# Hybrid encoder step on one core: the attention mask as one fp32r matmul, and the output projection's second column half token tile by token tile

## What is computed

```
x = x + 1/2 * SwiGLU_1(RMSNorm(x))
P = RMSNorm(x) @ w_in
A = gated delta rule, 4 heads of 128 (blocks of 128 tokens, then the streams)
B = softmax(q1 k1) v - lambda * softmax(q2 k2) v, 4 heads, two maps of dim 64 each
    prompt: a query of 64-token chunk c sees the keys of chunks 0..c
x = x + concat(A, B) @ w_out          (1024 x 1024)
x = x + 1/2 * SwiGLU_2(RMSNorm(x))
```

## Time and profile before

| | |
|---|---|
| median of three runs | 1503.07 us |
| the profiled execution | 1500.5 us, of which the span is 1498.7 us |
| mean granted clock of TensorE | 0.975 of full speed |
| busy: PE, VectorE, ScalarE, GpSimd | 1404.1, 914.1, 668.4, 360.7 us (94, 61, 45, 24%) |
| attention and delta rule, scores of the prompt | 774.6 to 875 us of the span |
| output projection | 993.4 to 1052.1 us |
| first product of the second FFN | 1061.57 us |

### The profile page before, as it was taken

How to read it: one execution, slowest core, us unless ns; L and a number is a source line. 1 busy time by engine, 2 the same in 40 slices (tenths; PEclk the granted TensorE clock), 3 DMA queues, 4 the chain that set the end, 5 groups by cost and what they waited for, 6 DMA issues and landing times.

```text
span 1498.7 us, 24413 instructions
## 1 busy us (share of the span) xinstructions
PE 1404.1 (94%) x8709; PEld 1259.7 (84%) x8709; DVE 914.1 (61%) x1485; ACT 668.4 (45%) x1253; POOL 360.7 (24%) x240
## 2 busy tenths in 40 slices
PE   5999999999997999999988988779899999999999
PEld 5999999988886997787877665467799999998887
DVE  4976677644446676647636665643787777654444
ACT  6555555533334544434243332442655555543333
POOL 0645555300000000312022221000265555530000
PEclk9999999999998999999998999899999999999999
DMA  6223332270102422101030025580112222235000
GB/s 191 63 88 91 89 92 86 84 267 0 28 0 60 126 79 64 57 30 56 33 124 1 1 76 187 185 297 1 57 57 85 84 84 84 84 108 228 6 30 35
DMA packets 139254, 127.27 MB, mean 85 GB/s; under 512 B 3781, under 2 KB 107845, under 8 KB 139196
## 3 DMA queue, kind: packets, MB, share of 16 engines
q1 hardware_dynamic: 136684, 117.15, 24.4%
q0 software_dynamic: 2512, 9.34, 1.8%
HBM read 115.83 MB, written 10.39 MB: 84 GB/s over the span
## 4 chain that ended last, share of the span: by engine, by line
PE 83%; DVE 11%; ACT 3%; issue 2%; DMA 1%; POOL 0%; SPq 0%; DVEq 0%; ACTq 0%
PE psum_all L898 22%; PE psum_all L899 21%; PE psum_all L900 21%; PE psum_all L908 6%; PE psum_all L1756 2%; DVE hw_lo L329 1%; PE psum_all L1769 1%; PE psum_all L2003 1%; PE psum_all L2006 1%; PE psum_all L1872 1%; PE psum_all L1761 1%; DMA x_tok<-x_prompt 1%; DVE x_norm L423 0%; PE psum_all L472 0%; DMA K_c<-cache_k 0%
## 5 line engine op out<-in xcount | busy, mean ns | idle before, releaser
L898 PE MATMUL psum_all<-hw_hi,gu_op 128*128 128x320 f32 x1200 | 375.6, 313 | 12.3 <-DVE gu_op L554 4.7
L899 PE MATMUL psum_all<-hw_lo,gu_op 128*128 128x320 f32 x1200 | 372.7, 311 | 0.0
L900 PE MATMUL psum_all<-hw_hi,gu_op 128*128 128x320 f32 x1200 | 372.3, 310 | 0.0
L898 PEld LDWEIGHTS psum_all<-hw_hi,gu_op 128*128 128x128 f32 x1200 | 228.3, 190 | 13.3 <-issue 8.9
L899 PEld LDWEIGHTS psum_all<-hw_lo,gu_op 128*128 128x128 f32 x1200 | 228.3, 190 | 0.0
L900 PEld LDWEIGHTS psum_all<-hw_hi,gu_op 128*128 128x128 f32 x1200 | 228.1, 190 | 0.0
L554 DVE TENSOR_TENSOR gu_op<-w_sum,gu_op 128x512 fp32r<-128x512 f32 x160 | 161.0, 1007 | 55.7 <-ACT gu_op L550 50.9
L779 POOL TENSOR_TENSOR w_sum<-raw_gu 128x512 f32<-128x512 f32 x80 | 137.8, 1722 | 214.0 <-DVE gu_op L554 210.8
L898 PE MATMUL psum_all<-wd_hi,a_hi 128*128 128x512 f32 x440 | 171.4, 390 | 1.7 <-DVE x_tok L916 1.7
L900 PE MATMUL psum_all<-wd_hi,a_lo 128*128 128x512 f32 x440 | 171.2, 389 | 0.0
L899 PE MATMUL psum_all<-wd_lo,a_hi 128*128 128x512 f32 x440 | 171.2, 389 | 0.0
(11 more groups left out here) (349 smaller groups left out, 2500.1 us busy)
## 6 DMA issues: line engine op xcount, KB each, us to landing
raw_gu<-ffn_w_gu SPq DMA_DIRECT2D x80, 512.0 KB, 4.6
wd<-ffn_w_down SPq DMA_DIRECT2D x2, 4096.0 KB, 20.9
raw_b<-w_in SPq DMA_DIRECT2D x8, 1024.0 KB, 5.3
K_c<-cache_k SPq DMA_DIRECT2D x8, 1024.0 KB, 8.1
V_c<-cache_v SPq DMA_DIRECT2D x8, 1024.0 KB, 5.5
wd<-ffn_w_down SPq DMA_DIRECT2D x2, 3584.0 KB, 11.9
raw_cv<-w_in SPq DMA_DIRECT2D x13, 512.0 KB, 4.0
wd<-ffn_w_down SPq DMA_DIRECT2D x6, 1024.0 KB, 5.0
```

The costliest lines, as they stand in the source:

```text
L898: nc.tensor.matmul(out, lhs_hi, rhs_hi, start=start, stop=False, skip_group_check=True)
L899: nc.tensor.matmul(out, lhs_hi, rhs_lo, start=False, stop=False, skip_group_check=True)
L900: return nc.tensor.matmul(out, lhs_lo, rhs_hi, start=False, stop=stop, skip_group_check=True)
```

## The change

The mask's operands become two fp32r tiles made once by ScalarE, and the mask is one fp32r matmul over the same 64 rows as the scores (the 64 rows add up to -6.4e31). The concatenated heads get tiles of their own, laid out by token tile (`mixed_hi`, `mixed_lo`, over the same memory as `hT_hi`, `hT_lo`). The first column half of the projection stays as it was. All weights of the second half are kept split (seven blocks in `keep_o`, the eighth in `o_hi[0]`), made in an order that interleaves them with the first half's (SPLITS); the second half then runs token tile by token tile, eight blocks of weights each, with the norm transposes of a tile behind the product of the next. The norm's steps on ScalarE and VectorE go in turn, tile by tile.

```diff
-            square(0)
-            square(1)
-            root(0)
-            square(2)
-            root(1)
-            root(2)
-            columns(0, 4)
+            if in_turn:
+                square(0)
+                root(0)
+                square(1)
+                root(1)
+                columns(0, 2)
+                square(2)
+                root(2)
+                columns(2, 4)
...
+            if in_turn:
+                dve.wait_ge(gain_ready, 16)
+                for t in range(3):
+                    residual(t)
+                    inverse(t)
+                    scale(t)
...
             token_lo(dve, f, 0)
             token_lo(dve, f, 1)
+            if in_turn:
+                residual(3)
             token_lo(dve, f, 2)
             token_lo(dve, f, 3)
...
+        late = Region(nc, gain_at + 4096, small.at)
+        late_neg = late.put("late_neg", [P, P], F32R)
+        late_one = late.put("late_one", [P, DK], F32R)
...
+            nc.scalar.activation(late_neg[:], const("early_neg"), ACT.Copy)\
+                .then_inc(N["qkT_copied"], 1)
+            nc.scalar.activation(late_one[:], const("ones")[:, 0:DK], ACT.Copy)\
+                .then_inc(N["qkT_copied"], 1)
...
-                    last = nc.tensor.matmul(psum[m][:, n - 64:n], const("early_neg")[0:1, :],
-                                            const("lvl64")[0:1, 64:P], start=False, stop=True,
+                    last = nc.tensor.matmul(psum[m][:, n - 64:n], late_neg[rows, :],
+                                            late_one[rows, :], start=False, stop=True,
...
+        SPLITS = [(0, 0), (0, 1), (0, 2), (1, 0), (0, 3), (1, 1), (0, 4), (1, 2), (0, 5), (1, 3),
+                  (0, 6), (1, 4), (0, 7), (1, 5), (1, 6), (1, 7)]
...
+            for half, k in SPLITS:
+                if half == 0:
+                    if k == 2:
+                        finish(diff_out_act(act, 1))
+                    for m in BEHIND.get(k - 2, ()):
+                        out_act(act, m)
+                    if k >= 2:
+                        act.wait_ge(N["wo_step"], k - 1)
+                elif k == 0:
+                    act.wait_ge(*on.tr(2 * TT))
+                elif k >= 5:
+                    act.wait_ge(N["wo_lo"], NTH_SPLIT[0, k if k == KT - 1 else 4])
+                    if k == KT - 1:
+                        act.wait_ge(N["wo_step"], KT - 1)
                 act.wait_ge(s_wo[half], 16)
-                nc.scalar.activation(o_hi[:, n % 2], raw_o[half][:, k, :], ACT.Copy)\
+                nc.scalar.activation(out_weights(half, k)[0], raw_o[half][:, k, :], ACT.Copy)\
                     .then_inc(N["wo_hi"], 1)
...
+            dve.wait_ge(N["x_back"], 32)
+            for t in range(TT):
+                wout_residual(dve, 0, t)
...
+        def late_bank(t):
+
+            return (7, 0, 1, 0, 1)[t]
...
+            for t in range(TT):
+                if t:
+                    pe.wait_ge(N["wo_res"], (0, 1, 2, TT + 2, TT + 3)[t])
+                for k in range(KT):
+                    if t == 0:
+                        pe.wait_ge(N["wo_lo"], NTH_SPLIT[1, k])
+                    last = three(psum[late_bank(t)], mixed_hi[:, t, k], mixed_lo[:, t, k],
+                                 *out_weights(1, k), k == 0, k == KT - 1)
+                last.then_inc(N["wo_out"], 1)
+                if 1 <= t <= 3:
+                    norm_pe(pe, f2.n, (t - 1,), f2.hx)
...
             wout_pe(pe)
-            norm_pe(pe, f2.n, range(3), f2.hx)
             ffn_pe(pe, f2)
```

More of the change, by code:

```diff
@@ L343, in columns @@
                         .then_inc(f.hx.sem, 1)
-            square(0)
-            square(1)
-            root(0)
-            square(2)
-            root(1)
-            root(2)
-            columns(0, 4)
+            if in_turn:
[7 more added lines that the diff above has]
+                columns(2, 4)
+            else:
+                square(0)
+                square(1)
+                root(0)
+                square(2)
+                root(1)
+                root(2)
+                columns(0, 4)
             token_hi(act, f, 0)
@@ L365, in ffn_norm_act, with ffn_norm_dve @@
             token_hi(act, f, 5)
-        def ffn_norm_dve(dve, f, gain_ready, residual=lambda t: None, ahead=lambda dve: None):
+        def ffn_norm_dve(dve, f, gain_ready, residual=lambda t: None, ahead=lambda dve: None,
+                         in_turn=False):
             s = f.n
@@ L370, in ffn_norm_dve @@
             scale = lambda t: norm_scale(dve, s, t)
[L371 to L381, removed]
+            if in_turn:
[4 more added lines that the diff above has]
+                    scale(t)
+            else:
+                residual(0)
+                residual(1)
+                inverse(0)
+                residual(2)
+                inverse(1)
+                dve.wait_ge(gain_ready, 16)
+                scale(0)
+                inverse(2)
+                scale(1)
+                scale(2)
+                residual(3)
             token_lo(dve, f, 0)
             token_lo(dve, f, 1)
+            if in_turn:
+                residual(3)
             token_lo(dve, f, 2)
@@ L2354, in out_hT @@
             half, t = n // TT, n % TT
-            part = which[:, 4 * half:4 * half + 4, t * P:(t + 1) * P]
+            part = which[:, t, 4 * half:4 * half + 4, :]
             return part if n < 2 * TT - 1 else part.rearrange("p h (b c) -> p h b c", c=32)
@@ L2376, in out_act, with out_weights @@
             act.wait_ge(*on.tr(n + 1))
-            nc.scalar.activation(out_hT(hT_hi, n), out_psum(n), ACT.Copy).then_inc(on.hi.sem, 1)
+            nc.scalar.activation(out_hT(mixed_hi, n), out_psum(n), ACT.Copy).then_inc(on.hi.sem, 1)
         def out_dve(dve, n):
             dve.wait_ge(*on.hi(n + 1))
-            V.tensor_tensor(out_hT(hT_lo, n), out_psum(n), out_hT(raw(hT_hi), n),
+            V.tensor_tensor(out_hT(mixed_lo, n), out_psum(n), out_hT(raw(mixed_hi), n),
                             ALU.subtract).then_inc(on.lo.sem, 1)
+        SPLITS = [(0, 0), (0, 1), (0, 2), (1, 0), (0, 3), (1, 1), (0, 4), (1, 2), (0, 5), (1, 3),
+                  (0, 6), (1, 4), (0, 7), (1, 5), (1, 6), (1, 7)]
+        NTH_SPLIT = {split: n + 1 for n, split in enumerate(SPLITS)}
+        keep_o = [nc.alloc_sbuf_tensor_at(f"keep_o{k}", [P, 2, BANK], F32R, offset=at)
+                  for k, at in enumerate([F0 + 4096 * i for i in range(5)] +
+                                         [tok_at + 4096 * i for i in range(2)])]
+        def out_weights(half, k):
+            if half and k < KT - 1:
+                return keep_o[k][:, 0], keep_o[k][:, 1]
+            return o_hi[:, 0 if half else k % 2], o_lo[:, 0 if half else k % 2]
         def wout_act(act):
@@ L2401, in wout_dve @@
                 out_dve(dve, n)
[L2402 to L2407, removed]
-                dve.wait_ge(N["wo_hi"], n + 1)
[L2409 to L2414, removed]
+            for n, (half, k) in enumerate(SPLITS):
+                if half == 0:
+                    if k == 2:
+                        finish(diff_out_dve(dve, 1))
+                    for m in BEHIND.get(k - 2, ()):
+                        out_dve(dve, m)
+                dve.wait_ge(N["wo_hi"], n + 1)
+                hi, lo = out_weights(half, k)
+                V.tensor_tensor(lo, raw_o[half][:, k, :], raw(hi), ALU.subtract)\
+                    .then_inc(N["wo_lo"], 1)
+            dve.wait_ge(N["x_back"], 32)
+            for t in range(TT):
+                wout_residual(dve, 0, t)
         def wout_residual(dve, half, t):
@@ L2426, in wout_pe @@
                 out_pe(pe, n)
-            for n in range(2 * KT):
-                half, k = n // KT, n % KT
-                if n == 0:
+            for k in range(KT):
+                if k == 0:
                     pe.wait_ge(*on.lo(TT))
-                elif n == KT // 2:
+                elif k == KT // 2:
                     pe.wait_ge(*on.lo(2 * TT))
-                pe.wait_ge(N["wo_lo"], n + 1)
+                pe.wait_ge(N["wo_lo"], NTH_SPLIT[0, k])
+                hi, lo = out_weights(0, k)
                 for t in range(TT):
[L2435 to L2444, removed]
-                    out_pe(pe, m)
+                    last = three(psum[t], mixed_hi[:, t, k], mixed_lo[:, t, k], hi, lo, k == 0,
+                                 k == KT - 1)
+                last.then_inc(N["wo_step"], 1)
+                for m in BEHIND.get(k, ()):
+                    out_pe(pe, m)
+            for t in range(TT):
+                if t:
+                    pe.wait_ge(N["wo_res"], (0, 1, 2, TT + 2, TT + 3)[t])
+                for k in range(KT):
+                    if t == 0:
[5 more added lines that the diff above has]
+                    norm_pe(pe, f2.n, (t - 1,), f2.hx)
         s_wo = [sem(f"w_out_loaded{i}") for i in range(2)]
```

25 lines of the change are left out of this document (11 added, 14 removed).

## The result

| | before | after |
|---|---|---|
| median (lowest to highest) | 1503.43 us (1500.19 to 1504.56, 4 runs) | 1479.21 us (1472.44 to 1481.6, 4 runs) |
| the profiled execution | 1500.5, span 1498.7, clock 0.975 | 1481.6, span 1479.8, clock 0.973 |
| PE busy | 1404.1 us | 1383.9 us |

The ratio of the times is 0.9843, with a 95% interval from 0.9819 to 0.9867: faster by 24.2 us in the medians and by 18.9 us in the two profiled executions. The forecast was 1485.4. The runs of after spread over 9 us, those of before over 4; the lowest had a granted clock of 0.983, the profiled one, the highest, of 0.973. What follows accounts for the profiled pair.

A forecast was written before the change was run, and what follows sets the result against it. PE bounds the kernel, holding 83% of the chain. Mask 7.5 - 0.6 wait + 9.5 projection and norms = 16.4 us off, giving 1484.1 from the profile or 1486.7 from the median; middle 1485.4, range 1479 to 1493.

The forecast's parts named there:

- the mask's term: Prompt attention: cheaper masks and second scores save 0.58 us a unit, 13 units on the chain, 7.5 us (2.1 to 11.2).
- The drain at a change of row count: Prompt attention on PE: changing tiling mode drains TensorE, 0.20 to 0.25 us at each change of row count.
- The freed time isn't eaten at once: Prompt attention: VectorE's combined probabilities are ready 1.5 us before PE asks, against 0.6 us saved per unit.
- Rival (b): Prompt attention: half of the gain returns as waits for VectorE and ScalarE, 1489.2 us; chance 0.13.
- (a): Prompt attention: mask weights not loaded under the scores, which keep their fixed part; gain 4.4 us, 1488.5 us; chance 0.13.
- (d): Prompt attention: fp32r mask takes as long as the pair; only the projection gains, 8.9 us, 1492.9 us; chance 0.04.
- The two copies at no cost: ScalarE ahead of the transposed q: two new copies, some 0.5 us, hidden while ScalarE waits for PE's first transposes.
- `raw_o[1]`: Projection's first half: this load, landing 15.0 us after issue, is due earlier; PE waits 0.6 us once (0 to 3).
- Rival (e): Projection, ScalarE's order: work queues behind the split awaiting `raw_o[1]`; landing at 1025 makes it slower, about 1508 us; chance 0.02.
- Second half and norms: Projection's second half to last `hx` copy: 40.4 instead of 49.9 us, 9.5 saved: 6.7 idle, 0.3 wait, 2.4 half clock.
- Rival (c): Projection's second half: norms don't keep up or the clock falls at the FFN's start; 3 us back, 1488.4; chance 0.05.
- The wait behind the last `hx`: Last `hx` to first combined operand: unchanged 22.8 us, ending in PE's 2.40 us wait for VectorE; whole block moves up.

The follow-up runs named there:

- run 3: Kernel before with the mask still float32 in two passes, but on the scores' 64 rows: 1489.73 us (one run).
- run 4: Kernel before with its one-row float32 masks, but both maps' scores ahead of both masks: 1496.29 us (one run).
- run 5: Kernel before with a one-pass fp32r mask over all 128 rows: 1496.8 us (one run).
- run 6: Kernel before with a one-pass fp32r mask on one row: 1495.9 us (one run).
- run 10: The changed kernel once more with no edit, five executions: 1477.74 us, ratio 0.9833 to before.
- run 7: Changed kernel with the norm transposes of tiles 0 to 2 behind the whole projection, ScalarE and VectorE still tile by tile: 1489.96 us (one run).
- run 8: Changed kernel with those transposes behind the whole projection and the old norm order on ScalarE and VectorE: 1490.2 us (one run).
- run 1: Kernel before with the new mask alone (two fp32r tiles, 64 rows, copies included): 1486.74 us, ratio 0.9905.
- run 11: Changed kernel with the first two combined FFN operands split ahead of the last token operand, measured again: 1473.84 us, ratio 0.9808 to before.
- run 9: Changed kernel with the first two combined FFN operands split ahead of the last token operand: 1475.85 us, ratio 0.981 to before.

## Why the prediction was right, and where its sum was wrong

- **Sign, range, total**: right, but that the median lies in the range, by 0.2 us, is in part luck: the low end of 1479 came from a mask gain of 11 us in which the maps still followed each other, and the mechanism that acted was another. The profiled execution is 2.5 us faster than the 1484.1 of the sum. Two errors of the mask's term, in opposite directions, leave +4.7 (12.2 - 7.5); 0.6 more came from the wait that didn't occur; the later start (1.15) and the cache stage (1.6) took 2.7 back.
- **The step that failed**: "Between the maps nothing changes mode any more, so the second scores lose their 0.20", and the upper bound of 0.86 a unit built on it. It assumed that the maps still follow each other and only a fixed part falls. Runs 3 to 6 show that with no one-row or full-height matmul between them the second scores lose all of their 1.06 us. A unit gains 1.74 us, not 0.58; over 16 units of four sizes PE's work falls by 19.3 us, 1.2 a unit. In run 10, at a higher granted clock, it falls by 23.7. The row that could have told was read for something else: 64 rows of contraction, map 0 on partitions 0 to 63 and map 1 on 64 to 127, is two disjoint halves of the array. (No run puts both maps on the same half.) The Trainium skill says it as well, in the sentence behind the one that the prediction used: TensorEngine Tiling (Array Packing), Key Properties, "Different tiles can execute LdWeights and Matmul in parallel". Here they do (four records in 1.13 us).
- **The drain at a change of row count**: right as a fact, wrongly placed in importance. The gap costs 0.2 to 0.25. Part of it shows in the scores: to the start of masks on the same rows they take 0.97 us (run 3), to that of one-row masks 1.06 (run 4). That a matmul of another row count also keeps the two halves from working at once costs 1.06.
- **"The freed time isn't eaten at once"**, with 1.5 us of slack against 0.6 a unit: it holds for savings of that size (the rows of one and of 128 rows in the table), not for 1.74. Rival (b) is partly true: 7.1 of 19.3 us, 37%, returned as waits, most of them for VectorE. It didn't decide since the saved work was larger than the rival's. The prediction named waits for VectorE between the units as a sign of being wrong, and by that sign it was.
- **Rivals (a) and (d)**: (a) wanted 1488.5 from an exposed load. The mask's loads begin at 844.43, under scores that began at 843.90 and last to about 845.0 on both halves, so neither load had a free half. The Trainium skill's TensorE: Matmul & The Clock Gate, What overlaps and what doesn't, lets a load run under a matmul only if the row groups differ. By that rule (a) would have come true. The trace doesn't agree: not here, and not in the earlier trace rows, where two loads on the same rows lie within 0.29 us under the scores. (d) is refuted: the fp32r step costs 0.22 or less against 0.36.
- **The two copies at no cost**: right. From the `z` copy to the first scores it is 15.26 us before and 15.25 after.
- **`raw_o[1]`**: the order on ScalarE and the split's wait (3.24 us) as told; it landed 14.4 us after its issue instead of 15.0, and PE's wait of 0.6 didn't occur. Rival (e), slower, would have needed 17 us more.
- **Second half and norms**: right by term. 30.8 us forecast and 30.8 measured; last `hx` ended at 40.5 for 40.4; gain 9.47 for 9.5. Rival (c) is refuted by a busy share of 100% and a clock of 1.00. Runs 7 and 8 show what it would have looked like: with the transposes at the end, the idle time and the half clock return.
- **The wait behind the last `hx`**: it moved up whole, as said; 21.99 and 21.97 us.

## What to carry to other kernels

If two matmuls of 64 rows lie on different halves of the array's rows, look at what stands between them in PE's program: one matmul of another row count makes them run one behind the other, and giving it the neighbours' rows, or only moving it behind both, may be worth a whole matmul. When a saving is several times what was reckoned, reckon the slack of the other engines anew: here a third of it came back as waits. And when a stage's results fan out per tile, put the consumer's short PE steps between the tiles' products; reordering the products alone brought a fifth.

## What was not expected of the hardware

**The granted clock moves a stage by 2.7 us.** Seven profiled executions have the new mask. In four of them (after, run 1, run 7, run 11) the attention stage took 108.98 to 109.02 us at a granted clock of 0.89, in three (runs 8, 9, 10) 106.27 to 106.30 us at 0.95. After and run 10 have the same code and agree to 0.1 us up to a wait of 1.94 us in both; what follows, in run 10 and then in after:
```profile
799.00 0.66 PE L1737 MATMUL psum_all<-consts,Xm 128*128 128x128 f32 x4 [1.94 <-DVE Xm L1605]
```
```profile
798.99 1.12 PE L1737 MATMUL psum_all<-consts,Xm 128*128 128x128 f32 x4 [1.94 <-DVE Xm L1605]
```
From 799 to 803 us the granted clock was 1.00 (2.4 GHz) in the one and 0.50 (1.2 GHz) in the other. The other five part in the same way at this place. Why the same wait was followed by either isn't shown. The 1.6 us of the cache stage is of the same kind: its work is the same in all thirteen profiled executions, and it took 108.4 to 112.9 us, at clocks from 0.94 down to 0.90. Its state product takes 3.21 us after, at a clock of 0.61, where it took 1.98 before at 1.00:
```profile
911.61 3.21 PE L1898 MATMUL psum_all<-u_exp,kd 128*128 128x512 f32 x4
```
```profile
922.24 1.98 PE L1872 MATMUL psum_all<-u_exp,kd 128*128 128x512 f32 x4
```
So a gain of the attention stage read from one pair of traces is good to about 2.7 us here (12.2 or 14.9 for the mask, by the execution that is taken), and the 5 us between the medians' gain (24.2) and the profiled pair's (18.9) needs no other cause; that it has none wasn't shown.

**An instruction on one number a partition takes 3.40 us.** VectorE's timeline, and POOL's beside it:
```profile
861.41 3.40 DVE L2083 TENSOR_TENSOR soft<-soft,lam 128x1 f32<-128x1 f32 x1
```
```profile
861.75 1.05 POOL L1715 TENSOR_TENSOR kbg<-tok,gates 128x512 f32<-128x512 f32 x1
862.75 1.04 POOL L1716 TENSOR_TENSOR tok<-tok,gates 128x512 f32<-128x512 f32 x1
863.75 1.04 POOL L1717 TENSOR_TENSOR kd<-tok,gates 128x512 f32<-128x512 f32 x1
```
It ends at 864.81, with POOL's third operation (864.79), and PE then waits 3.78 us for the combined probabilities at 866.17, the longest of the new waits. In most other units the same instruction takes 0.16 us. The Trainium skill's SBUF — State Buffer, SBUF: two separate sides, says that of a VectorE operation with two SBUF inputs and a GpSimd operation that reads SBUF, the one that starts first holds the port they share for its whole length, and the other is blocked. The rows agree in the common end. They don't show why VectorE lost, whose record begins 0.34 us ahead of POOL's first, nor why it stayed blocked over three operations. Before had the same 3.40 us (at 872.44, L2053), when more of it lay under PE's work: PE waited 2.05 us. Moving those three operations wasn't tried.
